# The opening of a three-block forward pass: GpSimd's first transfers wait for x, and the low-rank product moves between the halves of the first weight product

## The reference

```python
h = rmsnorm(x, norm_mix)                 # x [256, 1024]
proj = h @ w_in                          # w_in [1024, 3104]
q, k, v, g, r = split(proj, ...)         # r: the last 32 columns, 16 per direction
r_f, r_b = split(r, 2)
logits = (r_dir @ w_up + b_up)           # w_up [16, 512], one for each direction
log_a = log_sigmoid(logits) / 16
# then: a chunked scan with cumulative sums of log_a, q, k and v
```

## Time and profile before

| what | value |
|---|---|
| median of 3 runs | 1075.74 us (1074.56 to 1075.93) |
| the profiled execution's own time | 1075.9 us |
| its span in the profile | 1074.1 us |
| TensorE matmul busy | 1044.4 us (97%) |
| VectorE busy | 835.3 us (78%) |
| ScalarE busy | 614.7 us (57%) |
| GpSimd busy | 18.3 us (2%) |
| mean HBM read and write rate over the span | 155 GB/s |

### The profile page before, as it was taken

One profiled execution on the slowest core, in us unless ns is written; L12 is line 12 of the kernel. 1 busy time (PEld: TensorE's weight loads), 2 busy tenths in 40 slices (PEclk: granted clock), 3 DMA queues, 4 the chain that ended last, 5 costly groups with the idle time before them and its releaser, 6 DMA issues.

```text
span 1074.1 us, 25196 instructions
## 1 busy us (share of the span) xinstructions
PE 1044.4 (97%) x10822; PEld 996.0 (93%) x10822; DVE 835.3 (78%) x1378; ACT 614.7 (57%) x879; POOL 18.3 (2%) x38
## 2 busy tenths in 40 slices
PE   7999999999999999999999989999999999999997
PEld 6999999999999989999999978889999988889997
DVE  6964589888879776988788757889899999845473
ACT  7834565444546666644444567556667667676443
POOL 2000000000000000000000000000000000000000
PEclk9999999999999999999999999999999999999999
DMA  9553276666564515476765635233333322234531
GB/s 284 183 171 100 67 247 215 228 222 233 192 201 153 165 56 174 161 254 216 245 213 187 197 116 184 93 119 120 103 97 119 118 82 81 80 106 151 177 118 40
DMA packets 135927, 168.27 MB, mean 157 GB/s; under 512 B 3200, under 2 KB 125056, under 8 KB 135584
## 3 DMA queue, kind: packets, MB, share of 16 engines
q1 hardware_dynamic: 131936, 153.51, 44.0%
q0 software_dynamic: 3904, 13.50, 3.4%
HBM read 164.90 MB, written 2.10 MB: 155 GB/s over the span
## 4 chain that ended last, share of the span: by engine, by line
PE 86%; DVE 8%; ACT 4%; issue 1%; DMA 1%; SPq 0%; DVEq 0%; ACTq 0%
PE bank L312 18%; PE bank L313 16%; PE bank L314 16%; PE bank L633 2%; PE banks L635 2%; PE bank L635 2%; PE banks L631 2%; PE bank L631 2%; PE banks L633 2%; DVE hf L2449 2%; PE bank L1164 1%; PE banks L1132 1%; DVE wl L298 1%; PE bank L593 1%; PE bank L309 1%; PE bank L310 1%
## 5 line engine op out<-in xcount | busy, mean ns | idle before, releaser
L312 PE MATMUL bank<-xh,wh 128*128 128x256 f32 x1360 | 399.0, 293 | 0.6 <-DVE wl L274 0.6
L313 PE MATMUL bank<-xl,wh 128*128 128x256 f32 x1392 | 394.4, 283 | 0.0
L314 PE MATMUL bank<-xh,wl 128*128 128x256 f32 x1360 | 385.2, 283 | 0.0
L312 PEld LDWEIGHTS bank<-xh,wh 128*128 128x128 f32 x1360 | 260.4, 191 | 11.1 <-issue 4.1
L313 PEld LDWEIGHTS bank<-xl,wh 128*128 128x128 f32 x1392 | 267.0, 192 | 1.1 <-issue 1.0
L314 PEld LDWEIGHTS bank<-xh,wl 128*128 128x128 f32 x1360 | 260.6, 192 | 0.0
L274 DVE TENSOR_TENSOR wl<-raw,wh 128x2048 fp32r<-128x2048 f32 x95 | 216.9, 2287 | 47.3 <-ACT wh L269 47.1
L269 ACT ACTIVATE wh<-raw 128x2048 fp32r<-128x2048 f32 x95 | 181.0, 1906 | 38.6 <-PE bank L635 35.6
L298 DVE TENSOR_TENSOR wl<-raw,wh 128x1024 fp32r<-128x1024 f32 x86 | 103.8, 1218 | 23.2 <-ACT wh L290 23.1
L2449 DVE SCALAR_TENSOR_TENSOR hf<-big,vecs,hf 128x256 f32<-128x256 f32 x240 | 101.5, 479 | 0.0
L290 ACT ACTIVATE wh<-raw 128x1024 fp32r<-128x1024 f32 x86 | 87.6, 1057 | 11.2 <-PE bank L314 5.5
(11 more groups left out here) (405 smaller groups left out, 2212.7 us busy)
## 6 DMA issues: line engine op xcount, KB each, us to landing
raw<-in_ffn_w_up SPq DMA_DIRECT2D x44, 1024.0 KB, 5.1
raw<-in_w_in SPq DMA_DIRECT2D x36, 1024.0 KB, 5.4
raw<-in_ffn_w_down SPq DMA_DIRECT2D x22, 1024.0 KB, 5.0
big<-in_ada_w_t POOLq DMA_DIRECT2D x24, 512.0 KB, 5.3
raw<-in_gla_w_in SPq DMA_DIRECT2D x11, 1024.0 KB, 6.1
raw<-in_attn_w_qkv SPq DMA_DIRECT2D x6, 1024.0 KB, 5.0
raw<-in_gla_w_out SPq DMA_DIRECT2D x4, 1024.0 KB, 5.0
raw<-in_attn_w_out SPq DMA_DIRECT2D x4, 1024.0 KB, 5.1
```

Source lines behind the costliest of these rows:

```text
L312: nc.tensor.matmul(ps, wh, xh, start=start, stop=False)
L313: nc.tensor.matmul(ps, wh, xl, start=False, stop=False)
L314: return nc.tensor.matmul(ps, wl, xh, start=False, stop=stop)
```

## The change

Four edits, all in the opening:

1. GpSimd waits for `x_landed3` (the last quarter of x) before it issues `w_r`.
2. The eight `w_up` transfers count on a semaphore of their own, `w_up_c_landed`; TensorE waits for them (8 x 16) just before the gate logits, and VectorE waits for `w_r` alone (16). The row c counts on the same semaphore and is issued once the gate logits are done instead of once x is split; its wait for `rms_split` now stands behind it.
3. VectorE multiplies `w_r` with the norm weights after the low parts of both halves of block 0, no longer before them.
4. TensorE makes the low-rank product inside `first_product`, between its first 24 and its last 24 matmuls.

```diff
@@ gpsimd @@
+            pool.wait_ge(sem("x_landed3"), 16)
             pool.dma_start(w_r[:, :, :], a["gla_w_in"][:, 3072:3104].rearrange("(k p) n -> p k n", p=P))\
                 .then_inc(sem("rank_landed"), 16)
             pool.wait_ge(sem("w_up_zeroed"), 1)
             for j in range(4):
                 for d, name in enumerate(("gla_w_gate_up_f", "gla_w_gate_up_b")):
                     rows = slice(32 * j + 16 * d, 32 * j + 16 * d + 16)
-                    pool.dma_start(w_up[rows, d, :], a[name]).then_inc(sem("rank_landed"), 16)
+                    pool.dma_start(w_up[rows, d, :], a[name]).then_inc(sem("w_up_c_landed"), 16)
+            pool.wait_ge(sem("gate_logits"), 2)
+            pool.dma_start(SILU_C, a["c_row"].broadcast_to([P, D])).then_inc(sem("w_up_c_landed"), 16)
             pool.wait_ge(sem("rms_split"), 4)
-            pool.dma_start(SILU_C, a["c_row"].broadcast_to([P, D])).then_inc(sem("c_landed"), 16)
@@ tensor, first_product @@
                     elif k == KT // 2:
+                        rank_rows()
                         pe.wait_ge(w_lo_ready, N_GIN + 1)
@@ tensor @@
             sums(0, first_ones)
-            pe.wait_ge(sem("rank_on_dve"), 1)
-            for k in range(KT):
-                rows = slice(32 * (k % 4), 32 * (k % 4) + 32)
-                last = nc.tensor.matmul(PS[7][rows, 0:T], w_r[:, k, :], X[:, k, :], start=k < 4, stop=k >= 4,
-                                        skip_group_check=True)
-            last.then_inc(sem("rank_rows"), 1)
+            def rank_rows():
+                pe.wait_ge(sem("rank_on_dve"), 1)
+                ...
+                last.then_inc(sem("rank_rows"), 1)
             pe.wait_ge(sem("early_split"), 4)
             first_product()
             pe.wait_ge(sem("rank_on_dve"), 2)
+            pe.wait_ge(sem("w_up_c_landed"), 8 * 16)
@@ scalar, first feed-forward layer @@
-                    act.wait_ge(sem("c_landed"), 16)
+                    act.wait_ge(sem("w_up_c_landed"), 9 * 16)
@@ vector @@
-            dve.wait_ge(sem("rank_landed"), 9 * 16)
+            lo_by_halves(N_GIN)
+            dve.wait_ge(sem("rank_landed"), 16)
             v.tensor_tensor(w_r[:, :, :], w_r[:, :, :], spread(vec("norm_mix", 0, KT).unsqueeze(2), [P, KT, 32]),
                             ALU.mult).then_inc(sem("rank_on_dve"), 1)
-            lo_by_halves(N_GIN)
             dve.wait_ge(sem("rstd_ready"), 1)
```

More of the change, by code:

```diff
@@ L685, in _ @@
             sums(0, first_ones)
-            pe.wait_ge(sem("rank_on_dve"), 1)
-            for k in range(KT):
-                rows = slice(32 * (k % 4), 32 * (k % 4) + 32)
-                last = nc.tensor.matmul(PS[7][rows, 0:T], w_r[:, k, :], X[:, k, :], start=k < 4, stop=k >= 4,
-                                        skip_group_check=True)
-            last.then_inc(sem("rank_rows"), 1)
+            def rank_rows():
+                pe.wait_ge(sem("rank_on_dve"), 1)
+                for k in range(KT):
+                    rows = slice(32 * (k % 4), 32 * (k % 4) + 32)
+                    last = nc.tensor.matmul(PS[7][rows, 0:T], w_r[:, k, :], X[:, k, :], start=k < 4, stop=k >= 4,
+                                            skip_group_check=True)
+                last.then_inc(sem("rank_rows"), 1)
             pe.wait_ge(sem("early_split"), 4)
```

## The result

| kernel | median | lowest to highest | runs |
|---|---|---|---|
| before | 1075.19 us | 1074.22 to 1076.16 | 18 |
| changed | 1077.07 us | 1076.37 to 1078.17 | 18 |

The ratio is 1.0017, with a 95% interval of 1.0010 to 1.0023: 1.9 us slower. The kernel before has two groups of times in this set, nine executions from 1074.22 to 1074.71 us and nine from 1075.67 to 1076.16 us, and its median of 1075.19 us lies between them, where there is no execution. In the four later sets, 101 executions, its medians are 1075.72 to 1075.77 us; against those the changed kernel would be about 1.3 us slower. The profiled execution of the changed kernel took 1077.14 us, with a span of 1075.3 us; that of before took 1075.9 us with 1074.1 us.

What follows compares the result with a forecast made beforehand. The opening was taken as bound by the ScalarE and VectorE chain up to TensorE's start of block 4. Only the later low-rank product counted, +1.05 us on 1075.74 us, other terms zero: 1076.8 us, range 1075.1 to 1078.5 us.

Steps and rivals of the forecast that it cites:

- the wait that was named as the sign for it: VectorE, ahead of its scaling: idle for 1.5 to 2 us, with the low-rank product as releaser.
- Edit 1, 1.20 us: Opening: without GpSimd's transfers beside x, ScalarE's first split starts at 10.37 instead of 11.57 us, at most about 1.6 us gained.
- the raw blocks behind it: Block transfers in the opening: same bytes ahead of them as before, block 1 asked for 1 us later; price zero.
- Edit 4, the deciding term, +1.05 us: Opening: low-rank product behind 24 matmuls ends at 16.85 us, so VectorE's scaling starts 1.05 us later.
- When w_r and w_up arrive: Opening transfers: w_r lands by 14.6 us, w_up near 20 us at the latest; price zero, at most 0.3 us.
- rival E: Opening: w_r meets the blocks in the other queue, lands at 16 us, product 1.65 us late: 1077.4 us; chance 0.06.
- The gap and the clock: Ahead of block 4: TensorE stands 3.1 instead of 2.0 us, half-clock stretch costs the same; zero, within 0.5 us.
- Rival C: Ahead of block 0: TensorE's 1.55 us idle slows the clock and the 24 matmuls, +2.4 us, 1078.1 us; chance 0.17.
- Rival D: Opening: x's first quarter also comes earlier, block 0's first half lands by 9 us, not slower: 1075.3 us; chance 0.10.
- Rival B: Opening: block 0's first half is not earlier, low-rank rows come 2.2 us later: 1077.9 us; chance 0.12.

Runs made afterwards that it cites:

- e2: Changed kernel with w_r issued at once and only the eight w_up transfers behind the wait for x: 1077.21 us, ratio 1.0017.
- e3: Changed kernel with VectorE's scaling of the low-rank rows moved behind the fourth normed pair: 1075.13 us, ratio 0.9997.
- e1: Changed kernel without GpSimd's wait for x, so w_r and w_up travel beside x again: 1080.63 us, ratio 1.0046.
- f2: e1 with eleven throwaway matmuls filling TensorE's idle time between the sums of squares and block 0: 1078.51 us, ratio 1.0025.
- f1: Kernel before with only the transfers changed, w_r issued at once and w_up behind x's last quarter: 1075.99 us, ratio 1.0008.
- f3: Changed kernel with thirteen throwaway matmuls in the gap ahead of block 4: 1075.76 us, ratio 1.0003.
- h1: Changed kernel with twelve and fifteen throwaway matmuls in the gaps ahead of block 4 and the third part's first product: 1074.85 us, ratio 0.9993.
- g2: Kernel before with seven and fifteen throwaway matmuls in the gaps ahead of block 4 and the third part's first product: 1073.91 us, ratio 0.9986.
- e4: Changed kernel with VectorE's multiplication of w_r behind the second normed pair and its scaling behind the fourth: 1075.43 us, ratio 0.9999.

## Why the prediction was right, point by point

- **The number.** Forecast 1076.8 us, measured 1077.07 us. That is closer than the sum deserves. The forecast difference was 1.05 us and the measured one 1.88 us; the 0.8 us between them are mostly hidden because the base of the sum, 1075.74 us from three executions, came out of the upper of the two groups and lies 0.55 us above the median of this set.
- **The sign and the place.** Forecast: the low-rank product behind 24 matmuls holds up VectorE between its first two normed pairs, and the shift arrives whole at block 4. The changed profile shows the shift, but not the wait that was named as the sign for it: VectorE idles 0.40 us ahead of its scaling instead of 1.5 to 2 us, and 2.08 us one step earlier, for `w_r`. With `w_r` early (e2) the wait for the product is there as forecast, 2.05 us; e3 takes the wait away and 0.96 us of the shift with it; e1 and f2 keep the place and lose the transfers' gain, and are worse.
- **Edit 1, 1.20 us.** Under-sized, 1.60 us at ScalarE's first split in this profile (0.98 us in f1). The bound given was 1.6 us. Missed was what comes after: I priced the raw blocks behind it at zero because ScalarE asks for them later. With the low-rank wait gone that does not hold; f1 shows that blocks 1 and 2 take the gain back.
- **Edit 4, the deciding term, +1.05 us.** The place was right. The sum of steps was not the one that happened: the 24 matmuls were done by 15.4 us instead of 15.8 and then TensorE waited 0.44 us for `w_r`, so the product began at 15.96 instead of 15.78 us. That the two came out alike is luck: 0.42 us too little at the first matmul against 0.44 us of waiting that was priced at zero. Scaling +1.23 us on the chain's 15.86 us, block 4 +1.33 us; with both gaps filled, +1.12 us at block 4 and 0.94 us in the medians.
- **"When w_r and w_up arrive", price zero.** This step failed: "`w_r` is there at 13.4 us, at the latest at 14.6 us". It landed at 15.45 us, 7.7 us after its issue; this is the mechanism of rival E, at a smaller size. The slack of 1.7 us covered most of it: e2, with `w_r` early, gains 0.16 us at the low-rank product, and in f3 and h1, where the same order finds `w_r` 7.4 and 7.1 us after its issue, the product begins at 15.52 and 15.61 us without a wait. `w_up` landed by 18.6 us as forecast, 1.3 us before TensorE asked.
- **The gap and the clock, "zero, within 0.5 us either way".** This term was mis-sized, and in kind: the stretch itself costs the same in both kernels (1.3 us, above), but with the longer gap it stands there in more of the executions. Of the 1.88 us between the medians 0.94 us is the change itself (h1 against g2), and the executions with equal mean clock say the same: at 0.995 and 0.996 the changed kernel has 1076.87 us on average (13 executions) and the kernel before 1075.90 us (57). The rest, about 0.9 us in this set, goes by how many executions of each kernel are spared the stretch: none of 18 of the changed one, nine of 18 of the kernel before going by their times (half of 1.3 us is 0.6 us), 37 of 101 in the later sets. Against the medians of those sets only about 0.4 us are left for it. f3 agrees: filling that gap alone takes 1.3 us off the changed kernel. The remaining 0.3 us are likely the five executions of the changed kernel with a mean clock of 0.994: they lie 0.9 us above the others on average (1077.8 us), about the price of a doubled stretch behind the later gap, but no trace of one was kept.
- **Rival C** did not happen in the profiled execution of the changed kernel (TensorE's gap ahead of block 0 was 0.82 us instead of the 1.55 us that I had worked out, since the first matmul came 0.42 us earlier and the sums of squares ended 0.31 us later, at 11.59 us) and did in e1. With the low-rank product behind the 24 matmuls the chain is exposed to the clock in that product, where the kernel before was not. **Rival D** is refuted by the changed profile: the first split came 1.60 us earlier, more than the forecast 1.20 us, and nothing of it reached block 4. (The start of the squares, 4.69 instead of 4.88 us, says nothing: it lies between 4.3 and 5.0 us in the other profiles, whatever GpSimd does.) **Rival B** is refuted, the first split being early in all ten profiles with `w_up` behind x (9.6 to 10.6 us) and late in the four without (11.4 to 11.6 us in the kernel before, e1, f2 and g2).

## What to carry to other kernels

A small product in an idle gap cost nothing here; moved into a full stretch it delays whoever reads it by all that now stands before it, and an in-order engine that asks for it in the middle of its own list passes that delay on to everything behind. A transfer moved away from the front moves its bytes in front of something else: look for the next landing before booking the gain. And when two medians differ by more than the chain moved, hold TensorE's clock with fill in the gaps of both kernels and compare again: here that took the spread from 2.7 to 0.5 us in one kernel and from 1.8 to 0.8 us in the other, and left 0.94 of the 1.9 us to the change itself. Look at the distribution too: a median between two groups of times moves with their shares.

## What the runs showed of the hardware that was not expected

- Seven and fifteen short matmuls whose result is thrown away, in two gaps of 2.0 and 3.9 us, make this kernel 1.9 us faster in the medians and 1.6 us in the means (g2, 1073.91 us, ratio 0.9986, interval 0.9976 to 0.9995), with the granted clock at 1.00 in the stretches behind both. One low stretch costs 1.3 us behind the first gap and 0.6 to 0.7 us behind the second. Each of the short matmuls, 128 columns of float32, appears as two instructions and takes about 0.24 us (24 instructions in 2.84 us in h1).
- In the profiles the clock fell to its lower level behind the gaps ahead of block 4 of 2.00 us (before), 2.37 us (e4), 2.93 us (f1), 3.20 us (e2) and 3.21 us (changed), and did not behind the 1.69 us of e3. This is no sharp limit: by their mean clock and time, 37 of 101 executions of the kernel before were spared the stretch, with the same order of work.
- The landing of the same transfer varies with what is in the other queue: `w_r` took 5.1 to 6.0 us in the eight profiles where it goes beside x and 7.0 to 7.7 us in the six where it goes beside the weight blocks; the last `w_up` took 5.8 us before and 6.4 us in the changed kernel. The start of ScalarE's first work on x, which depends only on the first transfers, lay between 4.3 and 5.0 us in the profiles, so a single profile places the opening no better than that.
